# Depthwise convolution of a transformer kernel: shifted copies on two queues, one more pair of product tiles ahead of them, and 20 instead of 24 taps on TensorE

## What is computed

```python
def conformer_conv(h, w_pw1, b_pw1, w_dw, b_dw, ln_g, ln_b, w_pw2, b_pw2):
    u = h @ w_pw1 + b_pw1
    a, gate = jnp.split(u, 2, axis=-1)
    u = a * jax.nn.sigmoid(gate)
    u = jnp.pad(u, ((0, 0), (CONV_WIDTH - 1, 0), (0, 0)))      # CONV_WIDTH = 31
    u = lax.conv_general_dilated(u, w_dw[:, None, :], ...,      # one filter of 31 taps
                                 feature_group_count=D_MODEL) + b_dw   # for each channel
    u = jax.nn.silu(layer_norm(u, ln_g, ln_b))
    return u @ w_pw2 + b_pw2
```

## Time and profile before

| | us |
|---|---|
| median of 3 runs | 1782.29 (1776.49 to 1785.28) |
| the profiled execution | 1778.04 |
| its span in the trace | 1776.2 |
| its mean granted TensorE clock | 0.991 of full |
| PE busy | 1730.8 (97%) |
| DVE busy | 921.0 (52%) |
| ACT busy | 606.8 (34%) |

### The profile page before, as it was taken

How to read it: one execution, slowest core, us unless ns; L and a number is a source line. 1 busy time by engine, 2 the same in 40 slices (tenths; PEclk the granted TensorE clock), 3 DMA queues, 4 the chain that set the end, 5 groups by cost and what they waited for, 6 DMA issues and landing times.

```text
span 1776.2 us, 21979 instructions
## 1 busy us (share of the span) xinstructions
PE 1730.8 (97%) x8152; PEld 1377.6 (78%) x8152; DVE 921.0 (52%) x1231; ACT 606.8 (34%) x892; POOL 185.8 (10%) x158
## 2 busy tenths in 40 slices
PE   9998999999999979799999999999999999999998
PEld 7777888888888846467888888878777788888886
DVE  5575436663665356646542344347774654234432
ACT  4354334441444222245322122234353432122221
POOL 0110111110111101001210011100000121001111
PEclk9999999999999989999999999999999999999999
DMA  6211222243223244402232222222210232222221
GB/s 226 71 48 37 71 81 95 94 130 95 83 94 107 82 119 133 125 13 95 98 104 95 95 95 94 95 83 68 75 48 9 87 102 100 95 95 95 94 83 47
DMA packets 48883, 157.91 MB, mean 89 GB/s; under 512 B 7088, under 2 KB 7728, under 8 KB 48816
## 3 DMA queue, kind: packets, MB, share of 16 engines
q1 hardware_dynamic: 48672, 156.07, 27.0%
q10 hardware_dynamic: 144, 0.92, 0.1%
HBM read 146.14 MB, written 2.10 MB: 83 GB/s over the span
## 4 chain that ended last, share of the span: by engine, by line
PE 90%; DVE 5%; ACT 2%; issue 2%; SPq 1%; DMA 0%; DVEq 0%; ACTq 0%
PE bank L1121 26%; PE bank L1122 26%; PE bank L1123 25%; PE bank L1634 2%; PE bank L1272 1%; PE bank L1278 1%; PE bank L1273 1%; PE bank L1211 1%; PE bank L1165 1%; DVE w_lo L1875 1%; PE bank L1804 1%; SPq L524 0%; ACT w_hi L671 0%; PE bank L1199 0%; PE bank L1373 0%
## 5 line engine op out<-in xcount | busy, mean ns | idle before, releaser
L1875 DVE TENSOR_TENSOR w_lo<-w_raw,w_hi 128x1024 fp32r<-128x1024 f32 x269 | 347.1, 1292 | 318.9 <-ACT w_hi L671 195.9
L1121 PE MATMUL bank<-a_hi,w_hi 128*128 128x512 f32 x1156 | 456.8, 395 | 0.5 <-issue 0.4
L1122 PE MATMUL bank<-a_lo,w_hi 128*128 128x512 f32 x1156 | 454.2, 393 | 0.0
L1123 PE MATMUL bank<-a_hi,w_lo 128*128 128x512 f32 x1156 | 451.3, 390 | 0.0
L1122 PE MATMUL bank<-g_lo,w_hi 128*128 128x512 f32 x688 | 270.7, 393 | 0.0
L1121 PE MATMUL bank<-g_hi,w_hi 128*128 128x512 f32 x688 | 269.0, 391 | 0.0
L1123 PE MATMUL bank<-g_hi,w_lo 128*128 128x512 f32 x688 | 268.0, 390 | 0.0
L1121 PEld LDWEIGHTS bank<-a_hi,w_hi 128*128 128x128 f32 x1156 | 217.1, 188 | 57.7 <-issue 8.7
L1123 PEld LDWEIGHTS bank<-a_hi,w_lo 128*128 128x128 f32 x1156 | 217.1, 188 | 47.5
L1122 PEld LDWEIGHTS bank<-a_lo,w_hi 128*128 128x128 f32 x1156 | 217.3, 188 | 45.2 <-issue 0.7
L671 ACT ACTIVATE w_hi<-w_raw 128x1024 fp32r<-128x1024 f32 x153 | 160.0, 1050 | 195.5 <-PE bank L1123 187.3
(11 more groups left out here) (290 smaller groups left out, 1840.4 us busy)
## 6 DMA issues: line engine op xcount, KB each, us to landing
w_raw<-in_stream SPq DMA_DIRECT2D x269, 512.0 KB, 3.5
shifted<-u_pad SPq DMA_DIRECT2D x128, 66.5 KB, 2.0
h<-in_xT SPq DMA_DIRECT2D x8, 256.0 KB, 6.0
out<-h SPq DMA_DIRECT2D x8, 256.0 KB, 2.1
cst_b<-in_consts SPq DMA_DIRECT2D x1, 896.0 KB, 9.7
cst_b<-in_consts ACTq DMA_DIRECT2D x1, 896.0 KB, 6.3
tap_cols<-in_vectors SPq DMA_DIRECT2D x16, 29.8 KB, 1.8
cols<-in_vectors SPq DMA_DIRECT2D x1, 285.0 KB, 8.2
```

What stands on the lines that cost most here:

```text
L1121: pe.matmul(out, w0, x0, start=start, stop=False, skip_group_check=loose)
L1122: pe.matmul(out, w0, x1, start=False, stop=False, skip_group_check=loose)
L1123: return pe.matmul(out, w1, x0, start=False, stop=stop, skip_group_check=loose)
L1875: dve.tensor_tensor(w_lo[slot][:, :], w_raw[slot][:, :], f(w_hi[slot][:, :]), ALU.subtract)\
```

## The change

Five things change together:

1. 20 taps are stacked on PE instead of 24; DVE takes 10 instead of 6, ACT still one.
2. In `CONV_SEQ` the stacked taps of block k come after the pair of tiles k+2 instead of k+1; `add_pe_taps` moves back by one block on DVE in the same way.
3. The 16 shifted copies of a block are issued half by SP and half by ACT. ACT issues its eight between its wait for `u_ready` and `first_tap(k)`.
4. There are three buffers `shifted` instead of two, and the tap matrices `taps_w` go round in three slots instead of having eight. Both queues and `build_taps` wait for `tap_sums` of three blocks before.
5. On DVE five taps instead of three stand ahead of the second w_lo, one ahead of the gate as before, and four instead of two behind it.

```diff
-TAPS_STACKED = 24
-CONV_SEQ = [("u", 0), ("u", 1), ("t", 0), ("u", 2), ("t", 1), ("u", 3), ("t", 2), ("u", 4), ("t", 3), ("u", 5),
-            ("t", 4), ("u", 6), ("t", 5), ("u", 7), ("t", 6), ("t", 7)]
+TAPS_STACKED = 20
+CONV_SEQ = [("u", 0), ("u", 1), ("u", 2), ("t", 0), ("u", 3), ("t", 1), ("u", 4), ("t", 2), ("u", 5), ("t", 3),
+            ("u", 6), ("t", 4), ("u", 7), ("t", 5), ("t", 6), ("t", 7)]
...
+        def shifted_copies(queue, k, turns):
+            if k >= 3:
+                queue.wait_ge(tap_sums, k - 2)
+            for a in turns:
+                for g in range(P // GROUP):
+                    sh = (g + a) % SHIFTS
+                    queue.dma_start(shifted[k % 3][sh * GROUP:(sh + 1) * GROUP, g * RW:(g + 1) * RW],
+                                    u_pad[k % 4][g * GROUP:(g + 1) * GROUP, sh:sh + RW])\
+                        .then_inc(shifted_landed[k % 3], 16)
...
-                    shifted_copies(k)
+                    sp.wait_ge(u_ready, k + 1)
+                    shifted_copies(sp, k, range(SHIFTS // 2))
...
             def first_tap(k):
                 act.wait_ge(u_ready, k + 1)
+                shifted_copies(act, k, range(SHIFTS // 2, SHIFTS))
                 act.activation(T(cv, k), u_pad[k % 4][:, CONV_W - 1:], ACT.Identity,
...
             def build_taps(k):
+                if k >= 3:
+                    dve.wait_ge(tap_sums, k - 2)
...
                 if k:
                     build_taps(k - 1)
-                if k >= 2:
-                    add_pe_taps(k - 2)
-                tap_ops(k - 1, 0, 3)
+                if k >= 3:
+                    add_pe_taps(k - 3)
+                tap_ops(k - 1, 0, 5)
                 lo_ahead(n + 1)
                 glu_in(k, 1)
-                tap_ops(k - 1, 3, 4)
+                tap_ops(k - 1, 5, 6)
                 glu(k)
-                tap_ops(k - 1, 4, taps_dve)
+                tap_ops(k - 1, 6, taps_dve)
             build_taps(KD - 1)
             tap_ops(KD - 1, 0, taps_dve)
+            add_pe_taps(KD - 3)
             add_pe_taps(KD - 2)
             add_pe_taps(KD - 1)
```

More of the change, by code:

```diff
@@ L250, in program @@
         RW = SEQ + TAPS_STACKED - SHIFTS
-        taps_w = sb("taps_w", [P, KD * TAP_COLS], where=big)
+        taps_w = sb("taps_w", [P, 3 * TAP_COLS], where=big)
         TW4 = (KD - 1) * CONV_W + TAPS_STACKED - SHIFTS + 1
@@ L254, in program @@
         unit_32 = sb("unit_32", [P, GROUP], where=big)
-        shifted = [sb(f"shifted{i}", [P, P // GROUP * RW], where=big) for i in range(2)]
+        shifted = [sb(f"shifted{i}", [P, P // GROUP * RW], where=big) for i in range(3)]
         big.close()
@@ L385, in program @@
         taps_built = sem("taps_built")
-        shifted_landed = [sem(f"shifted_landed{i}") for i in range(2)]
+        shifted_landed = [sem(f"shifted_landed{i}") for i in range(3)]
         dw_tap = sem("dw_tap")
@@ L514, in _ @@
             rounds = (N_RING - RING) // RING
-            def shifted_copies(k):
-                sp.wait_ge(u_ready, k + 1)
-                if k >= 2:
[L520 to L526, removed]
             conv_first, conv_last = (UNIT0["pw1"] + 7) // RING - 1, (UNIT0["pw1"] + 22) // RING - 1
@@ L1626, in conv_taps @@
                 pe.wait_ge(taps_built, k + 1)
-                pe.wait_ge(shifted_landed[k % 2], 256 * (k // 2 + 1))
+                pe.wait_ge(shifted_landed[k % 3], 256 * (k // 3 + 1))
                 if k >= 4:
@@ L1632, in conv_taps @@
                     for g in range(P // GROUP):
-                        c, o = k * TAP_COLS + (t * P // GROUP + g) * GROUP, g * RW + SHIFTS * t
+                        c, o = k % 3 * TAP_COLS + (t * P // GROUP + g) * GROUP, g * RW + SHIFTS * t
                         last = pe.matmul(conv_bank(k)[g * GROUP:(g + 1) * GROUP, :], taps_w[:, c:c + GROUP],
-                                         shifted[k % 2][:, o:o + SEQ], start=(t == 0),
+                                         shifted[k % 3][:, o:o + SEQ], start=(t == 0),
                                          stop=(t == TAPS_STACKED // SHIFTS - 1), skip_group_check=True)
@@ L2214, in glu @@
                     dve.wait_ge(last_tap, k - 3)
-                    dve.wait_ge(shifted_landed[k % 2], 256 * (k // 2 - 1))
+                    dve.wait_ge(shifted_landed[(k - 4) % 3], 256 * ((k - 4) // 3 + 1))
                 dve.scalar_tensor_tensor(u_pad[k % 4][:, CONV_W - 1:], tmp[b][:, 0:SEQ],
@@ L2253, in build_taps @@
                 dve.wait_ge(taps_landed, 256)
-                dve.tensor_tensor(T(taps_w, k, TAP_COLS).rearrange("p (t g c) -> p t g c", g=P // GROUP, c=GROUP),
+                if k >= 3:
+                    dve.wait_ge(tap_sums, k - 2)
+                dve.tensor_tensor(T(taps_w, k % 3, TAP_COLS).rearrange("p (t g c) -> p t g c", g=P // GROUP, c=GROUP),
                                   unit_32.rearrange("p (t g c) -> p t g c", t=1, g=1).broadcast_to(shape),
```

## The result

The changed kernel takes 1787.42 us, the kernel before 1781.03 us (medians of 20 runs each). The ratio is 1.0035, with a 95% interval of 1.0023 to 1.0047: slower by 0.35%, about 6 us. One of the changed kernel's 20 runs took 3476.59 us, nearly twice as long as any other; it is in the median (1786.11 us without it), not in the ratio. The forecast was 1784 us, 1.4 us more than before, in a range of 1771 to 1815.

The account below looks back on a forecast made before the run. PE bounds the kernel now; the gate, ACT and w_lo loop was to take over the stage. Its end, 728.4 + 64i, was 768.7 us, +1.4 us: 1782.3 + 1.4, about 1784 us, range 1771 to 1815.

Parts of the forecast that it names:

- the loop of gate, ACT's issues, w_hi and w_lo: Convolution stage: DVE's and ACT's loop takes over from PE once a lap exceeds 15.6 us, from i = 0.32 us.
- Lap 13.02 + 8i: DVE, one glu's end to the next: 13.02 us plus ACT's eight copy issues at pitch i each.
- 1.54 us for two taps ahead of the gate: DVE's lap: two more taps ahead of the gate, 0.77 us each, lengthen the loop by 1.54 us.
- i = 0.63 us: ACT's queue: pitch of one copy issue, taken from SP's for the same copy; makes the 64i term 40.3 us.
- the sum: End of the convolution stage: 728.4 + 64i, giving 768.7 us, or +1.4 us.
- the case that I held likeliest: Copy issues: queues independent at about SP's pitch, 0.57 to 0.70 us, for -2 to +6 us; chance 0.50.
- PE's savings turn into waits: PE in the stage: 1 to 3 us for w_lo ahead of odd tiles, about 9 us before blocks 6 and 7's taps.
- No wait ahead of block 0's taps, and 4.5 us for them: PE's timeline: the 11.5 us wait at block 0's taps goes, and they run at full clock in 4.5 us.
- A generator used in turn: Copy issues: one descriptor generator serves both queues in turn, ACT's part takes 16 pitches, +26 to +42 us; chance 0.20.
- a part of it shared: Copy issues: the queues hinder each other by 0.25 us, i up to 0.88, end 784.7, +17 us; chance 0.17.
- The free case, -30 us: Stage: issues don't hold up ACT's next instruction, PE stays the bound, end at 737.3, -30 us; chance 0.05.

Follow-up runs that it names:

- e1: The changed kernel with all 16 copies of a block issued by SP and none by ACT; ratio 0.9882 to the kernel before, stage 117.4 us.
- e9: The changed kernel with ACT's w_hi and first tap both moved ahead of its eight copies; ratio 0.9844 to the kernel before, stage 110.5 us.
- e3: The changed kernel with 24 taps stacked and six on DVE, all ahead of the gate; ratio 1.0036 to the kernel before, stage 147.7 us.
- e10: The changed kernel with DVE's ten taps split four ahead of the gate and six behind; ratio 0.9989 to the kernel before, stage 136.6 us.
- e6: The changed kernel with ACT's first tap ahead of its eight copies, w_hi still behind; ratio 1.0005 to the kernel before, stage 140.9 us.

## Why the prediction was right, and where it was off

- **The bound moves to the loop of gate, ACT's issues, w_hi and w_lo.** Right, and shown: removing the issues (e1) or what stands behind them (e9) takes 29 to 36 us off the stage, removing the four taps behind the gate (e3) takes nothing.
- **Lap 13.02 + 8i.** Right. ACT's steady bursts are 5.34 us to the start of the next instruction, i = 0.667, which makes 18.36; measured 18.30. With four issues 15.7, measured 15.7 to 15.8. The 1.54 us for two taps ahead of the gate is confirmed by e10 (1.5 us a lap).
- **i = 0.63 us.** This is the term that was mis-sized. SP's pitch was the right row to go to, but ACT's is 0.667, and two of eight bursts hold a long issue: 7.05 us in the first and 6.51 us in the fourth. The sum of the eight, each from its first issue to the start of the tap behind it, is 45.6 us against 40.3, +5.3 us. Put into the sum: 728.4 + 45.6 - 0.6 for the earlier first gate = 773.4, measured 772.35. The missing 1.1 us is mostly the third lap, which I had said would be up to 0.7 us shorter. So of the 5.7 us by which the stage is longer, 1.4 was forecast, 5.3 is this term, and 1.1 goes off again. The mean over all 64 issues is 45.6/64 = 0.713 us, just outside the 0.57 to 0.70 us of the case that I held likeliest; that the time still came out in the range, at +6 us, owes something to how wide it was. The burst of the kernel before that I read the pitch from (10.05 us) was one of the short ones. This one is as much of the same line:

```profile
677.34 11.40 SPq L524 DMA_DIRECT2D shifted<-u_pad  x16
```

The eight bursts of the kernel before last 84.5 us; with 0.04 us behind each that is 0.663 us for each of 128 issues. This mean would have made the term 42.4 us and the forecast +3.5 us. The rest is ACT's own pitch, which the kernel before doesn't show.
- **PE's savings turn into waits.** Right in kind: 10.9 us for w_lo, and 9.4 and 8.9 us ahead of the taps of blocks 6 and 7 ("about 9 us each"). Three details were not foreseen: the stacked taps start 18.3 us apart only between blocks 3 and 5 (694.29 to 730.94), before that 15.6 to 18.8 and at the end 13.9 and 15.4 us; the waits for w_lo are 0.5 to 4.2 us, not 1 to 3, and the longest wait for w_lo, 4.2 us, is already at tile 5, as the first burst on ACTq is the long one; and block 6's taps are released by DVE's tap matrix, not by the copies. The last two are the same lateness of DVE.
- **No wait ahead of block 0's taps, and 4.5 us for them.** Right: 643.37, 4.50 us, no idle.
- **A generator used in turn, or a part of it shared.** Wrong as rivals: the pitch on SP didn't move. Only the long issues fall on both queues at once, and the two in the changed kernel add 2.9 us to ACT's bursts, where the forecast for turns was +26 to +42 us at the end of the stage. They held 0.37 of the chance and all of the upper part of the range.
- **The free case, -30 us.** As a forecast of the change it was rightly small. As a price it met the number by luck. e9, in which the issues don't hold w_hi or the tap up, has a stage 30.3 us shorter than the kernel before, but PE isn't its bound: the last gate ends 94.1 us after the first, when DVE has done its seven laps, and not the 92.0 us of the forecast (718.6 - 626.56). The stage then ends 16.4 us behind that gate and not 18.75, as the sum had left 5.04 us of waiting behind eight issues in a case that has no such wait. The two errors cancel.

## What to carry to other kernels

In this kernel DMAs issued by ACT cost it their issue time (0.67 us for such a copy), and everything behind them in program order waited. Before splitting a burst of issues over two queues, write down what stands behind it on the second engine and who waits for that; here moving two instructions ahead of the eight issues turned 0.35% slower into 1.6% faster. And when a lap has work on both sides of the instruction that it waits at, it is the side ahead of the gate that sets the lap: moving two taps behind the gate took 9.8 us off the stage (e10), while taking away the four behind it took nothing off (e3). Last, take a pitch from the mean of all bursts that a trace has, not from one.

## What the runs showed of the hardware

- ACT's issues don't slow SP's: a copy of 32 rows from SBUF to SBUF is issued in 0.59 us (median) on SP alone and beside ACT. On ACT, always beside SP, the median is 0.61 to 0.62 us and a steady burst of eight takes 5.34 us, 0.667 each against 0.63. In the steady bursts of the changed kernel ACT's second issue takes 0.87 us (the one at 699.03, for example), SP's 0.59.
- Issues on ACT overlap with the ACTIVATE ahead of them: in e6 the first issue starts 0.01 us after the first tap does, and in e9's steady bursts 0.02 to 0.03 us before it (718.82 and 718.84 for block 7). What stands behind the issues is held up.
- Now and then one issue takes 1.0 to 2.3 us instead of 0.6, two to four times in a kernel's stage. Where both queues are in the middle of a burst it holds both, to the same instant (15 of 15). What causes it stayed open; no run was made for it. Two such issues made 2.9 us of the difference between forecast and result.
